# A hybrid block on one core: the index projection changes places with the context's keys and values

## The reference, cut to what matters

```python
x = x + 0.5 * swiglu(rms_norm(x, ffn1_norm), ...)          # first block
h = rms_norm(x, mix_norm)
q, k, v, qi, ki, wi, u = split(h @ w_in)     # 512, 512, 512, 256, 64, 4, 512 columns
qi, ki = rope(qi), rope(ki)                  # index queries (4 heads) and keys, 32 of 64 columns rotate
score = sum over heads of wi * relu(qi . ki)               # causal
idx = top_k(score, 128)                                    # keys that a query may see
attn = softmax attention of rotated, normed q, k over idx
pooled = (mean of the last 2, 4, 8, 16 tokens - token) @ pool_w * pool_scale
x = x + concat(attn, pooled) @ w_out
x = x + 0.5 * swiglu(rms_norm(x, ffn2_norm), ...)
# second block: its context's keys and values need only ctx, c_ctx and weights
h_c = ctx * (1 + mods_c[1]) + mods_c[0]                    # 256 tokens
k_a, v_a, k_b, v_b = h_c @ w_in_2[...] + b_in_2[...]       # k_b then goes through an RMS norm
```

## Time and profile before

| | |
|---|---|
| median of 3 runs | 1744.66 us (1739.44 to 1745.13) |
| span of the profiled execution | 1744.9 us |
| mean granted clock of PE | 0.995 of 2.4 GHz |
| PE, weight load, DVE, ACT, POOL busy | 1709.5, 1390.8, 983.6, 661.9, 930.9 us |
| DMA | 178.39 MB, 102 GB/s over the span |

### The profile page before, as it was taken

One profiled execution on the slowest core, in us unless ns is written; L12 is line 12 of the kernel. 1 busy time (PEld: TensorE's weight loads), 2 busy tenths in 40 slices (PEclk: granted clock), 3 DMA queues, 4 the chain that ended last, 5 costly groups with the idle time before them and its releaser, 6 DMA issues.

```text
span 1744.9 us, 24492 instructions
## 1 busy us (share of the span) xinstructions
PE 1709.5 (98%) x8123; PEld 1390.8 (80%) x8123; DVE 983.6 (56%) x1515; ACT 661.9 (38%) x1374; POOL 930.9 (53%) x755
## 2 busy tenths in 40 slices
PE   8999999999999999999999999999998999999997
PEld 7888888888877888888888888864477988888887
DVE  4258645768985467252124429478778673542544
ACT  5322222243566432223223323766532642332333
POOL 4554453567972445544444545477953665544541
PEclk9999999999999999999999999999999999999998
DMA  7354452534211446433332433000122234333321
GB/s 229 114 174 152 145 157 85 175 97 127 73 49 49 125 141 193 145 97 96 115 91 82 118 97 96 25 1 25 49 79 66 62 99 142 96 91 103 96 84 49
DMA packets 279967, 178.39 MB, mean 102 GB/s; under 512 B 6537, under 2 KB 258629, under 8 KB 279749
## 3 DMA queue, kind: packets, MB, share of 16 engines
q1 hardware_dynamic: 265620, 149.36, 29.7%
q10 hardware_dynamic: 14256, 27.87, 4.7%
HBM read 175.11 MB, written 2.10 MB: 102 GB/s over the span
## 4 chain that ended last, share of the span: by engine, by line
PE 89%; DVE 7%; issue 1%; ACT 1%; DMA 1%; POOL 0%; DVEq 0%; SPq 0%; ACTq 0%; POOLq 0%
PE ps L971 87%; DVE mod_acc L2337 2%; PE ps L1453 1%; DVE hidH L2829 1%; DVE hidL L2830 0%; DVE mA L2828 0%; DVE stat L2654 0%; DVE ps L2680 0%; PE ps L1278 0%; PE ps L1403 0%; DMA xnat<-in_x 0%; DMA mod_raw<-in_w_mod 0%; DVE mA L2825 0%; DVE mB L2826 0%; POOL wL L804 0%
## 5 line engine op out<-in xcount | busy, mean ns | idle before, releaser
L804 POOL TENSOR_TENSOR wL<-raw,wH 128x512 fp32r<-128x512 f32 (+2 forms) x560 | 748.7, 1360 | 716.3 <-ACT wH L1766 705.0
L971 PE MATMUL ps<-actH,wH 128*128 128x512 f32 (+1 forms) x1312 | 510.6, 389 | 2.6 <-POOL actL L858 1.9
L971 PE MATMUL ps<-actH,wL 128*128 128x512 f32 (+1 forms) x1312 | 503.6, 384 | 0.0
L971 PE MATMUL ps<-actL,wH 128*128 128x512 f32 (+1 forms) x1248 | 480.0, 385 | 0.0
L1766 ACT ACTIVATE wH<-raw 128x512 fp32r<-128x512 f32 (+2 forms) x558 | 311.2, 608 | 329.2 <-PE ps L971 329.1
L971 PEld LDWEIGHTS ps<-actH,wH 128*128 128x128 f32 x1312 | 247.1, 188 | 53.3 <-issue 2.4
L971 PEld LDWEIGHTS ps<-actH,wL 128*128 128x128 f32 x1312 | 246.4, 188 | 48.9
L971 PE MATMUL ps<-hidH,wH 128*128 128x512 f32 (+1 forms) x720 | 268.6, 373 | 4.4 <-DVE hidL L2830 4.4
L971 PEld LDWEIGHTS ps<-actL,wH 128*128 128x128 f32 x1248 | 235.1, 188 | 47.0 <-DVE actL L2302 0.8
L971 PE MATMUL ps<-hidH,wL 128*128 128x512 f32 (+1 forms) x720 | 267.1, 371 | 0.0
L971 PE MATMUL ps<-hidL,wH 128*128 128x512 f32 (+1 forms) x720 | 267.0, 371 | 0.0
(11 more groups left out here) (378 smaller groups left out, 2044.1 us busy)
## 6 DMA issues: line engine op xcount, KB each, us to landing
mod_raw<-in_w_mod ACTq DMA_DIRECT2D x24, 1024.0 KB, 6.3
raw<-in_w_in SPq DMA_DIRECT2D x48, 512.0 KB, 3.7
raw<-in_ffn_w_up SPq DMA_DIRECT2D x44, 512.0 KB, 3.8
raw<-in_w_up SPq DMA_DIRECT2D x44, 512.0 KB, 3.8
raw<-in_ffn_w_gate SPq DMA_DIRECT2D x43, 512.0 KB, 3.8
raw<-in_ffn_w_down SPq DMA_DIRECT2D x32, 512.0 KB, 4.0
raw<-in_w_out SPq DMA_DIRECT2D x16, 512.0 KB, 3.9
raw<-in_w_down SPq DMA_DIRECT2D x16, 512.0 KB, 3.9
```

What stands on the lines that cost most here:

```text
L804: nc.gpsimd.tensor_tensor(wL[:, b:b + w // 2], raw[:, b:b + w // 2], wH[:, b:b + w // 2].bitcast(F32), ALU.subtract).then_inc(lo_ready, 1)
L971: return nc.tensor.matmul(out, a, b, start=first, stop=last)
```

## The change

`idx` goes ahead of `ctxkv` in the list of stages and on every engine. PE waits in `idx` for the rows of x block by block; `row_sums(1)` moves into the third slab of `idx` and uses bank 3 in place of bank 4. `spread_rows(1, 7)` and `idx_turns` move ahead of the first slab of `pool`, and the twelve scores stand behind steps 6 to 17 of `pool` in place of 20 to 31. DVE makes the tables and the index rotations before it drains `ctxkv`; the norm of the context's keys and the negated sink go behind the first attention, ahead of the drains of `out1`. The picks are dealt out anew: all of `pick(2)` and two rounds of `pick(3)` before the scales of k, six rounds after them, three after the rotation of q, and five in the attention.

```diff
     ffn("f1", ...)
+    rows("idx", w_in, 3 * ATT, IDX_COLS, 2)
     stage("ctxkv", 4, SLAB, ...)
-    rows("idx", w_in, 3 * ATT, IDX_COLS, 2)
     columns("pool", w_in, 3 * ATT + IDX_COLS, 4)
...
+    SCORES_FROM = 6
-    PICK_AT = range(2, 22, 2)
+    PICK_AT = (5, 9, 13, 17)
...
-                if st["name"] == "idx":                            # POOL
-                    pool.wait_ge(slab_done, stage_of["ctxkv"]["base"])
+                if st["name"] == "ctxkv":
+                    pool.wait_ge(slab_done, stage_of["idx"]["base"])
                     pool.wait_ge(lo_ready, st["base"] * 2)
                     zero_halves(qiT, S, qi_zero)
...
+        def before_idx():                                          # PE
+            pe.wait_ge(mod_cols, 7)
+        def idx_sums(j):
+            if j == 2:
+                row_sums(1, 3)
+        token_tiles("idx", IDX_COLS, 4, before_idx, tiles=KT, inside=idx_sums)
         st = stage_of["ctxkv"]
         for j in range(SLOTS):
...
-                if (j, kk) == (2, 2):
-                    row_sums(1)
...
+                    if k == 0 and b == 3:
+                        pe.wait_ge(rn_ready, 2)
...
-        def before_idx():
-            pe.wait_ge(act_ready, 2 * KT)
-            pe.wait_ge(rn_ready, 2)
-            pe.wait_ge(mod_cols, 7)
-        token_tiles("idx", IDX_COLS, 4, before_idx)
...
         st = stage_of["pool"]
+        pe.wait_ge(drained_a, drain_base["idx"] + 4)
+        pe.wait_ge(rn_ready, 2)
+        spread_rows(1, 7)
+        idx_turns()
         for j in range(SLOTS):
...
-                if j * KT + k >= 2 * KT + 4:
-                    idx_score(j * KT + k - (2 * KT + 4))
-            if j == 0:
-                pe.wait_ge(drained_a, drain_base["idx"] + 4)
-                spread_rows(1, 7)
-            if j == 1:
-                idx_turns()
+                if 0 <= j * KT + k - SCORES_FROM < (ST - 1) * IDX_HEADS:
+                    idx_score(j * KT + k - SCORES_FROM)
...
-        slabs("ctxkv", 0, nothing)                                 # ACT
         token_stage("idx", 4, pi, IDX_COLS)
+        slabs("ctxkv", 0, nothing)
...
+        act.wait_ge(idx_T, 1)
+        for half in (lower, upper):
+            nc.scalar.activation(kiT[half, :], ps[0:DH, 6, :], ACT.Copy).then_inc(idx_keys, 1)
         for j in range(SLOTS):
-            if j == 3:
-                relus(4, 12)
+            relus(*(min(max(KT * n - SCORES_FROM, 0), (ST - 1) * IDX_HEADS) for n in (j, j + 1)))
...
-        row_scale(1, RMS_EPS)                                      # DVE
+        row_scale(1, RMS_EPS, 3)
-        (drains of ctxkv into kctx, vA, vB)
-        (norm of kb, negated sink: 17 instructions)
         gained_tables(...)
         (rotation of the four tiles of pi, scaling of wi)
+        (drains of ctxkv into kctx, vA, vB)
         rows_spread(1, 7)
...
         pick(1)
-        pick(2, 0, 11)
+        pick(2)
+        pick(3, 0, 2)
...
         head_scales(1, 0, k_scale[:], (k_scaled, 1))
-        pick(2, 11)
-        pick(3, 0, 2)
+        pick(3, 2, 8)
...
-        pick(3, 2, 5)
+        pick(3, 8, 11)
...
         first_attention()
         (hidL of the attention's four tiles)
+        (norm of kb, negated sink: 17 instructions)
         last_down("out1", 1.0, "ffn2_norm", 2 * KT, 2 * KT, 2 * KT, ACC_TOTAL[1])
```

More of the change, by code:

```diff
@@ L977, in split_product, with row_sums @@
             return product(out, wl, xh, False, last)
[L979 removed]
+        def row_sums(n, b=4):
             pe.wait_ge(acc_done, ACC_TOTAL[n])
             for q in range(ST):
[L983 removed]
+                mm = product(ps[:, b, q:q + 1], acc[:, q * P:(q + 1) * P], ones[:, 0:1], True, True)
             mm.then_inc(row_sum, 1)
@@ L1917, in _ @@
             split(stage_of["k"], 0, j)
[L1918 to L1922, removed]
         token_stage("k", 4, k1, ATT, wait=(idx_rel_used, 12))
@@ L2271, in rsqrt, with row_scale, row_root @@
                     link(ins)
-        def row_scale(n, eps):
+        def row_scale(n, eps, b=4):
             dve.wait_ge(row_sum, n)
[L2276 to L2280, removed]
+            link(V.tensor_scalar(small[:, 0:ST], bank(b, ST), eps, None, ALU.add))
+            row_root(n, b)
+        def row_root(n, b=4):
+            rsqrt(rn[:], small[:, 0:ST], ST, last=(rn_ready, n + 1), room=bank(b, ST, 64) if n else None)
         def rows_spread(n, b=5):
@@ L2469, in _ @@
                 last_down("f1_down2", 0.5, "mix_norm", KT, KT, KT, ACC_TOTAL[0])
-        row_scale(1, RMS_EPS)
+        row_scale(1, RMS_EPS, 3)
         dve.wait_ge(misc_in, MISC_DMAS * 16)
[L2475 to L2494, removed]
         def gained_tables(cos, sin, gain, groups, half):
@@ L2524, in _ @@
         link(V.tensor_scalar(wi, wi, IDX_SCALE, None, ALU.mult))
+        kc = kctx[:].rearrange("p (q v b d) -> p q v b d", q=CT, v=NKV, b=2)
+        for g, v in ((0, vA), (1, vB)):
+            dve.wait_ge(slab_done, stage_of["ctxkv"]["base"] + 2 * g + 2)
+            for q in range(CT):
+                b = 2 * g + q
+                link(V.tensor_tensor(kc[:, q, :, g, :], bank(b, P).rearrange("p (v d) -> p v d", d=DH),
+                                     biasx[:, g * 256:g * 256 + P].rearrange("p (v d) -> p v d", d=DH), ALU.add))
+                V.tensor_tensor(v[:, q * P:(q + 1) * P], bank(b, P, P), biasx[:, g * 256 + P:g * 256 + 256],
+                                ALU.add).then_inc(drained_v, 1)
         rows_spread(1, 7)
@@ L2588, in during1 @@
             if n in PICK_AT:
-                pick(3, 6 + PICK_AT.index(n), 7 + PICK_AT.index(n))
+                pick(3, 12 + PICK_AT.index(n), 13 + PICK_AT.index(n))
         def rest_of_v(n):
             if n == 1:
-                pick(3, 5, 6)
+                pick(3, 11, 12)
                 for q, (done, count) in ((1, (v_block, 2)), (3, (slab_done, stage_of["v"]["base"] + SLOTS))):
@@ L2725, in _ @@
             V.tensor_tensor(tile(hidL, k), bank(AT1_BANK[k]), tile(hidH, k).bitcast(F32), ALU.subtract).then_inc(hid_ready, 1)
+        dve.wait_ge(drained_v, drain_base["ctxkv"] + 4)
+        kb = kctx[:].rearrange("p (n b d) -> p n b d", b=2, d=DH)[:, :, 1, :]
+        tk = tA[:, 0:2 * P].rearrange("p (n d) -> p n d", d=DH)
+        link(V.tensor_tensor(tk, kb, kb, ALU.mult))
+        link(V.tensor_reduce(small[:, 0:4], tk, AX_X, ALU.add))
+        link(V.tensor_scalar(small[:, 0:4], small[:, 0:4], 1.0 / DH, QK_EPS, ALU.mult, ALU.add))
+        rsqrt(small[:, 128:132], small[:, 0:4], 4)
+        link(V.tensor_tensor(kb, kb, small[:, 128:132].unsqueeze(2).broadcast_to([P, 4, DH]), ALU.mult))
+        V.tensor_tensor(kb, kb, gain2[:, DH:].unsqueeze(1).broadcast_to([P, 4, DH]), ALU.mult).then_inc(kctx_ready, 2)
+        dve.wait_ge(kctx_ready, 2)
+        link(V.tensor_scalar(sink[:, NH:], sink[:, 0:NH], -1.0, None, ALU.mult))
         last_down("out1", 1.0, "ffn2_norm", 2 * KT, 2 * KT, 2 * KT, ACC_TOTAL[1])
```

## The result

The changed kernel takes **1749.95 us** (median of 12 runs, 1744.70 to 1751.99); the kernel before, run beside it, 1743.76 (12 runs, 1738.88 to 1746.37). The ratio is 1.0036, with an interval of 1.0025 to 1.0047: slower by about 6 us, with 4.4 to 8.2 inside the interval. The forecast was 1751.7 with a range of 1743 to 1755.

The account below looks back on a forecast made before the run. PE, busy 98% of the span, was taken as the bound. Profiled span 1744.9 + 5.8 (wait) + 1.7 (clock) - 0.5 (attention) = 1751.9, against the median 1751.7 us; range 1743 to 1755.

Parts of the forecast that it names:

- The wait on pi: At the index turns: PE waits from 409.4 to 415.2 for DVE's index rotations, 5.8 us; range 3.5 to 6.6.
- DVE's 22: Before the index turns: 6 table and 16 rotation instructions of DVE, each reading two operands from SBUF.
- Ten of DVE's for ten of POOL's: Before the index turns: one DVE instruction passes per POOL subtraction, ten at 1.39 us, ending at 413.7.
- The lock: At SBUF's common port: a DVE instruction with two SBUF inputs waits out the whole POOL instruction; DVE ends at 415.2.
- sharing: Alternative at the port: each of the 22 takes about twice as long, DVE ends near 409.4, PE does not wait.
- nothing between: DVE's rotations in the trace take either 0.32 or 1.30 us, with no value in between.
- The clock: Behind the wait at the index turns: one piece of half clock, 1.7 us; bounds none and 3.3.
- The relief in the attention: First attention: six fewer pick rounds, 8 us less for DVE, gain 0.5 us from the wait for hidL.
- the attention was DVE's: Rival, 508 to 545: fewer picks also end the round trips and PE keeps its clock, up to 7.9 us; chance 0.07.
- Clock 1.00 there: Sign against the forecast: the first attention at clock 1.00 with few probT waits; before, the mean clock was 0.91.
- all that follows moves as a whole: From the index turns to the attention: stages are full at full clock, so the 5.8 us wait is not given back.
- Costed at nothing: The moved norm of the context's keys, SP's queue, the act_ready waits by blocks and the context's later drains: no cost.

Follow-up runs that it names:

- kernel 2: The changed kernel with the 16 index rotation instructions reading one operand from PSUM; 1743.64 us, 0.9995 of the kernel before.
- 3: The changed kernel with GpSimd's subtractions for the context's and pooling projection's slabs cut from 512 to 64 columns; 1742.51 us, ratio 0.9988 to the kernel before.
- kernel 4: The changed kernel with 18 extra matmuls on PE between the spreading and the index turns, filling the wait; 1749.12 us, ratio 1.0030 to the kernel before.
- 9: kernel 8 with the rope tables also made before the wait for the row sums; 1742.91 us, ratio 0.9987 to the kernel before.
- 10: Kernel 9 with the third tile's picks dealt as in the kernel before; 1744.03 us, ratio 1.0005 to the kernel before.
- Kernel 8: kernel 2 with DVE's two tiles of query rotations also read from PSUM; 1742.49 us, ratio 0.9993 to the kernel before.
- kernel 5: The kernel before with only the norm of the context's keys moved behind the first attention; 1744.06 us, ratio 1.0006 to the kernel before.
- kernel 7: The changed kernel with spreading and index turns again behind the pooling projection's first slab, scores eight products later; 1744.29 us, 0.9995 of the kernel before.
- 1: The changed kernel with the six rope tables made before DVE waits for the row sums; 1748.64 us, ratio 1.0023 to the kernel before.
- 6: The changed kernel with the third tile's picks dealt as in the kernel before; 1751.55 us, ratio 1.0034 to the kernel before.

## Why the prediction was right

The sum was +5.8, +1.7 and -0.5, 7.0 us; measured was 6.2 between the medians. The mechanism was the one forecast. That the sum came so close is partly luck: a wait that was put 1.7 us too long stands against 0.9 us that was missed. Its steps:

- **The wait on pi: right in kind, too long by 1.7.** 4.1 us and not 5.8. Everything came 1.5 us earlier than the marks that were used, since the stage ahead ended earlier; counted from there, DVE ended 1.5 us sooner than forecast and PE was ready 0.2 later. The term that was mis-sized is POOL: its ten took 1.29 us each, not 1.39, which is 1.0 of the 1.7 us, and its pause was 2.2 us, not 1.3, so that six of DVE's 22 went through it and not three, and three were left behind the ten and not five, another 0.4. Ten of DVE's for ten of POOL's was exact. Timing POOL by the spacing of its starts, as the Trainium skill advises ("Perfetto Trace Analysis", section "GPSIMD Engine Instruction"), would have given 5.1 and been nearer.
- **The lock.** The forecast chose between waiting out whole POOL instructions and sharing, by which each would take about twice its own time. The changed kernel's rows show the first: alone one of 128x80 takes 0.26 us and one of 128x160 0.32, beside POOL 1.24 and 1.3, as long as POOL's own 1.29. That is what the Trainium skill states ("SBUF — State Buffer", section "SBUF: two separate sides"), and the trace agrees. Kernels 2 and 3 show what ends the hold: with an operand in PSUM, or a short POOL instruction, the same work takes 0.32 to 0.48 us. The forecast's "nothing between" is too strong: a hold lasts for what is left of POOL's instruction, and a table of 128x256 that took 0.43 us in the pause took 0.75 at 392.78.
- **The clock: 1.7 forecast, 1.7 by the stretches, 1.5 by kernel 4.** The two pieces in before's attention, which the forecast also read as 1.7 each, cost about 1.3 each there, where PE waits in any case.
- **The relief in the attention: 0.5 forecast, 0.67 by kernels 9 and 10.** The 8 us less of DVE's work came as forecast (34.9 to 26.6). Whether it also spares falls of the clock is open. The rival "the attention was DVE's" needed 5.2 us; the eight probT waits stood as before. Clock 1.00 there had been named as a sign of error; it was seen, but without the few probT waits that went with it.
- **Missed: the query turn, +0.86.** The prediction took it that "all that follows moves as a whole". It does not: POOL's chain of pooling and keys moved further than the rest. Its subtractions for the first slab of k's weights went from 415.51 to 423.28, 7.8 us, and the last step of the key rotation that DVE meets from 488.39 to 494.26, 5.9 us; DVE's query rotations went from 489.83 to 494.19, 4.4 us. So they lie beside more of POOL's work. Kernel 8 shows that it is the same hold.
- **Costed at nothing:** the norm (4.5 us, hidden, kernel 5), the index stage's early start and the context's drains held: no wait of PE names them.
- **Its arithmetic.** The lower end of the range of the wait, 3.5 us, was given without a working, and two ends were rounded outward (1747.7 to 1747, 1756.3 to 1757). None of this changes the forecast.

Put together: 4.1 + 1.7 + 0.9 - 0.7 = 6.0 against 6.2. The agreement is closer than the medians allow one to say: against those of the kernel before beside the experiments, 1744.72 and 1745.16, the changed kernel is 5.2 and 4.8 us slower. Kernel 2 gives the first two terms back, kernel 8 the third.

## What to carry to other kernels

When a step is pulled ahead of work that stood between a producer and its wait, count the producer's queue by what runs beside it, not by its own durations: beside GpSimd's subtractions, VectorE's rotations with two operands in SBUF went one for each of GpSimd's. If the order is wanted, leave one operand where TensorE put it: the rotation straight from the PSUM bank cost no more instructions and took the loss away. And after a stall has shifted one engine, look at the next place where two engines meet; it need not shift by the same amount.

## What the runs showed of the hardware beyond that

- Beside the same POOL subtractions an instruction of DVE with an operand in PSUM kept its 0.32 to 0.39 us (128x160), and POOL's ten took 12.54 us instead of 12.91. But two operands in SBUF are not the only case that is held: the negated sink, a tensor_scalar of 128x8 that reads one operand from SBUF, took 1.31 us beside POOL and 0.17 where POOL rested (experiment 5). The picks' search for the eight largest reads one operand from SBUF too and was not held: 0.69 us for 128x512 beside POOL (kernel 7, 483 to 491), 689 ns on the average in the attention.
- Not every wait of PE is followed by a fall of the clock. Behind the wait on pi (3.2 to 4.1 us) it fell in all three profiles that have it unfilled (the changed kernel, 1 and 6). Behind a wait of 1.7 us between 1157 and 1171, which all twelve profiles have, it fell in six and stayed at 1.00 in the other six. So pieces of half clock come and go with the run; kernel 2's in the attention reads 0.63 and 0.80 over two stretches of 3 us.
- The stretch from the output projection's first matmul to the start of the last matmul of all, whose code is the same but for the norm, took between 1164.0 and 1171.5 us over the twelve profiles. Most of that is the wait of the earlier trace rows: in nine profiles PE stands there for 1.5 and 2.8 us, released by hidL, and the clock falls, and the stretch took 1169.3 to 1171.5; in kernels 1, 2 and 5 PE stands for 0.9 us and the clock holds, and it took 1164.0 to 1165.8. What decides between the two is not known. The times of the kernel before fall into two groups as well (1738.88 to 1740.26 and 1742.86 to 1746.37); that this wait parts them is not shown. One profiled run can misjudge a change of 6 us: here the two spans differ by 3.8.
